# Prompt attention: the two half additions of a finished output move from VectorE to GpSimd

## The reference

```python
o_c = jnp.einsum('bqkgn,bnkd->bqkgd', p_c.astype(vc.dtype), vc)      # compressed blocks
...
o_s = jnp.einsum('bqkgm,bkqmd->bqkgd', p_s.astype(vs.dtype), vs)     # selected blocks
...
o_w = jnp.einsum('bqkgw,bwkd->bqkgd', p_w.astype(vw.dtype), vw)      # sliding window of 512
return gates[..., 0:1] * o_c + gates[..., 1:2] * o_s + gates[..., 2:3] * o_w
```

## Time and profile before

| what | before |
| --- | --- |
| median of 3 runs | 1908.28 us |
| lowest and highest | 1908.01, 1908.91 us |
| span of the profiled execution | 1907.2 us |
| PE busy over the span | 97% |
| DVE, ACT, POOL busy over the span | 61%, 48%, 25% |
| prompt attention | about 714 to 1199 us of the span |
| in 720 to 1200 us: PE, DVE, ACT, POOL busy | 465.78, 437.71, 410.18, 262.20 us of 480 |

### The profile page before, as it was taken

One profiled execution on the slowest core, in us unless ns is written; L12 is line 12 of the kernel. 1 busy time (PEld: TensorE's weight loads), 2 busy tenths in 40 slices (PEclk: granted clock), 3 DMA queues, 4 the chain that ended last, 5 costly groups with the idle time before them and its releaser, 6 DMA issues.

```text
span 1907.2 us, 31779 instructions
## 1 busy us (share of the span) xinstructions
PE 1856.5 (97%) x11644; PEld 1663.7 (87%) x11645; DVE 1164.8 (61%) x1628; ACT 917.4 (48%) x1536; POOL 481.8 (25%) x643
## 2 busy tenths in 40 slices
PE   8999999999999999999999999999989999999997
PEld 8999988899999988889888898998857888888884
DVE  5544355642212359998999989644467587644756
ACT  3243330211210358888888888311123576645755
POOL 0000000000000215555555554002111244322333
PEclk9999999999999979999999999999988999999998
DMA  5234252232313410000000000524254798877865
GB/s 173 82 109 120 78 173 56 67 113 89 113 52 86 133 31 1 1 2 1 2 2 1 2 2 12 173 72 174 83 211 159 276 393 293 293 280 238 317 225 189
DMA packets 113735, 232.60 MB, mean 122 GB/s; under 512 B 25034, under 2 KB 81906, under 8 KB 107442
## 3 DMA queue, kind: packets, MB, share of 16 engines
q1 hardware_dynamic: 106162, 205.81, 30.5%
q0 software_dynamic: 7456, 25.17, 5.2%
HBM read 190.33 MB, written 42.71 MB: 122 GB/s over the span
## 4 chain that ended last, share of the span: by engine, by line
PE 53%; DVE 4%; ACT 3%; issue 1%; POOL 1%; DMA 0%; ACTq 0%; POOLq 0%; DVEq 0%
PE ps L3020 20%; PE ps L2069 6%; PE ps L2048 5%; PE ps L2690 5%; PE ps L254 4%; PE ps L2023 3%; PE ps L2025 3%; PE ps L3008 1%; DVE small L2133 1%; PE ps L2015 1%; PE ps L3069 1%; ACT turned_high L2238 1%; PE ps L2074 1%; PE ps L2676 1%; ACT region_w L2227 1%
## 5 line engine op out<-in xcount | busy, mean ns | idle before, releaser
L2133 DVE TENSOR_REDUCE small<-ps 128x1 f32<-128x640 f32 (+7 forms) x256 | 179.8, 703 | 26.3 <-PE ps L2015 24.4
L2157 DVE TENSOR_TENSOR turned_low<-ps,turned_high 128x512 fp32r<-128x512 f32 (+2 forms) x304 | 176.6, 614 | 12.0 <-ACT turned_high L2238 8.4
L2312 POOL TENSOR_SCALAR region_w<-region_w,small,gates 128x640 f32<-128x640 f32 (+7 forms) x172 | 141.7, 834 | 131.5 <-DVE small L2137 131.5
L2238 ACT CAST turned_high<-ps 128x512 fp32r<-128x512 f32 (+2 forms) x304 | 155.0, 531 | 31.6 <-PE ps L2048 28.2
L2023 PE MATMUL ps<-key_stacks,query_stacks 128*128 128x256 f32 (+3 forms) x384 | 142.0, 370 | 15.9 <-ACT region_w L2227 8.7
L2069 PE MATMUL ps<-turned_high,value_stacks 128*128 128x256 f32 (+1 forms) x608 | 152.1, 286 | 0.0
L2069 PE MATMUL ps<-turned_low,value_stacks 128*128 128x256 f32 (+1 forms) x608 | 142.2, 279 | 0.0
L2227 ACT ACTIVATE region_w<-ps,small 128x640 f32<-128x640 f32 (+7 forms) x172 | 121.7, 708 | 24.8 <-DVE small L2133 20.1
L3020 PE MATMUL ps<-gate_parts,rows_parts 128*128 128x512 f32 x552 | 131.7, 394 | 0.0
L3020 PE MATMUL ps<-down_parts,hidden_parts 128*128 128x512 f32 x552 | 131.1, 393 | 0.0
L3020 PE MATMUL ps<-up_parts,rows_parts 128*128 128x512 f32 x552 | 128.9, 389 | 0.0
(11 more groups left out here) (507 smaller groups left out, 4978.0 us busy)
## 6 DMA issues: line engine op xcount, KB each, us to landing
region_k<-in_w_gate SPq DMA_DIRECT2D x16, 2048.0 KB, 9.6
region_k<-in_w_up SPq DMA_DIRECT2D x16, 2048.0 KB, 10.1
region_w<-in_w_down SPq DMA_DIRECT2D x16, 2048.0 KB, 12.7
region_w<-in_w_in SPq DMA_DIRECT2D x16, 512.0 KB, 4.3
small<-gate_a SPq DMA_DIRECT2D x8, 516.0 KB, 3.4
region_w<-gate_b SPq DMA_DIRECT2D x8, 516.0 KB, 3.8
region_k<-in_x_prompt SPq DMA_DIRECT2D x8, 512.0 KB, 8.1
region_k<-in_w_in SPq DMA_DIRECT2D x8, 512.0 KB, 4.4
```

The lines of the kernel that those rows point to most:

```text
L2133: nc.vector.tensor_reduce(nmax[:, n % 4:n % 4 + 1], sc, AX.X, ALU.max, negate=True).then_inc(s_max, 1)
L2157: nc.vector.tensor_tensor(lo, m.ps[:, turn_bank(G), 0:w], hi, ALU.subtract).then_inc(s_lo, 1)
L2238: nc.scalar.copy(hi, m.ps[:, turn_bank(G), 0:w]).then_inc(s_hi, 1)
L2312: nc.gpsimd.tensor_scalar(probs(H, t), probs(H, t), rec[:, H % 4, t:t + 1], m.gates[:, 2 * p + t, col:col + 1], ALU.mult, ALU.mult).then_i ...
```

## The change

The two additions of each output leave VectorE's program and enter GpSimd's. On GpSimd they stand at the same H, behind `scale(H + 1)` and `queries`, and each is followed by a wait for its own completion (a stop). The first of them signals a new semaphore `s_o0`, the second `s_o`. Before the first stand waits for GpSimd's own latest scaling and its own latest low part of queries. The last output is likewise added by GpSimd, behind its loop, and no longer by VectorE behind `low_outputs(4)`.

```diff
-    s_pv, s_ot, s_o = lw.s_values, lw.s_half, lw.s_output
+    s_pv, s_ot, s_o, s_o0 = lw.s_values, lw.s_half, lw.s_output, m.sem("a_output_low_rows")
...
-        def output(n):
-
-            j, p, _, _ = half(4 * n)
-            at, _ = queries_at(p, j)
-            dve.wait_ge(s_ot, n + 1)
-            for g in range(NKV):
-                last = nc.vector.tensor_tensor(m.RO[rows[g], at], out_kept[rows[g], g * 256:g * 256 + 256],
-                                               m.RO[rows[g], at], ALU.add)
-            last.then_inc(s_o, 1)
-
...
-            if H >= 6 and H % 4 == 2:
-                output(H // 4 - 1)
...
-        output(NHALF // 4 - 1)
...
+        def output(n):
+
+            j, p, _, _ = half(4 * n)
+            at, _ = queries_at(p, j)
+            pool.wait_ge(s_ot, n + 1)
+            nc.gpsimd.tensor_tensor(m.RO[LO, at], out_kept[LO, 0:256], m.RO[LO, at], ALU.add).then_inc(s_o0, 1)
+            pool.wait_ge(s_o0, n + 1)
+            nc.gpsimd.tensor_tensor(m.RO[HI, at], out_kept[HI, 256:512], m.RO[HI, at], ALU.add).then_inc(s_o, 1)
+            pool.wait_ge(s_o, n + 1)
+
...
             if refill(H):
                 queries(refill(H)[1], refill(H)[0])
+            if H >= 6 and H % 4 == 2:
+                pool.wait_ge(s_scaled, scaled_of[H + 1, 1] + (scaled_behind(H + 1) is not None))
+                if refill(H):
+                    pool.wait_ge(s_ql, 4 * (refill(H)[0] - 1) + refill(H)[1] + 1)
+                output(H // 4 - 1)
+        output(NHALF // 4 - 1)
```

## The result

The changed kernel takes 1930.03 us in the median of four runs (1926.77 to 1931.37), beside 1908.6 (1908.01 to 1910.76) of the kernel before on the same chip. The ratio is 1.0105, interval [1.0091, 1.012], so 20 us more. That it would be slower was forecast, and by 13.1 us, with a range that ended at 1929. The profiled execution is the one of 1931.37 us.

The account below looks back on a forecast made before the run. TensorE was taken as nearly full, VectorE close behind, with GpSimd's scaling already last at some turns. 6.3 + 6.5 + 1.0 - 0.7 = 13.1 us brought the span to 1920.3, the median to 1921.4; range 1909 to 1929.

Parts of the forecast that it names:

- VectorE's relief: Work ahead of row maxima: 0.65 us at A, 0.24 at B, 6.5 in all, swallowed; rival that it is passed on, 0.09.
- Price of an output: On GpSimd behind the queries: two additions of 0.73 us and three stops of 0.09, 1.73 in all.
- 0.35 given back: GpSimd's scaling ahead of the new additions gets 0.35 us shorter at each place once VectorE's additions leave.
- Place A: First of four output places in a head: next scaling 1.05 us late, TensorE loses all, 6 times, 6.3.
- later waits "give nothing back": Behind the turn at A: waits shift along and recover nothing; rival that 0.9 of each 1.05 is recovered, 0.12.
- the collision with L2126: Rival at A: VectorE's L2126 meets the delayed scaling, 0.35 us each, 2.1 more, at most 4.1; above 1929 us, 0.06.
- Place B: Second output place in a head: next scaling 0.93 us late, no slack, TensorE loses 0.93, 7 times, 6.5.
- Place C: Third output place in a head: next scaling 0.42 us late, slack 0.28, TensorE loses 0.14, 7 times, 1.0.
- D: Fourth output place in a head: GpSimd idles 2.77 us before its next scaling, more than 1.73, so no loss.
- the last head: Head j = 7, no queries behind A and B: gains 0.45 us at A and 0.24 at B, 0.7 together.
- The last output: Behind GpSimd's loop: the 0.95 us wait goes, GpSimd needs 1.64 where VectorE needed 0.85; gain and loss cancel, 0.
- the case above it: Tail above 1929 us, chance 0.06; additions of 1.05 us each would give 1934.

Follow-up runs that it names:

- e1: The kernel before with the two additions of each output left out on every engine: ratio 0.9898, attention 6.6 us shorter; its whole time can't be used.
- e4: The changed kernel with L2126, the subtraction of the compressed scores' row maximum, replaced by a tiny operation for odd jobs: 1924.71 us, ratio 1.0079.
- e2: The kernel before, VectorE's additions kept, plus equal additions with stops on GpSimd at the change's places, into a spare buffer nobody reads: 1928.24 us, ratio 1.0092.
- e10: The changed kernel with only the last output put back on VectorE: 1928.19 us, ratio 1.0103.
- e3: The changed kernel with GpSimd's additions one pass later (H % 4 == 3) at all four places of a head: 1918.53 us, ratio 1.0046.
- e8: The changed kernel with one GpSimd addition of 128 rows per output, without its own-instruction waits there, and ScalarE copying in two shifted pieces: 1913.59 us, ratio 1.0016.
- e6: The kernel before with VectorE's additions moved behind the pass's second row maximum and its compressed sum: 1921.89 us, ratio 1.0067.
- e5: The changed kernel with GpSimd's additions one pass later, behind the scaling, at A, B and C, unchanged at D: 1905.77 us, ratio 0.9982.

## Why the prediction was right or wrong

- **VectorE's relief, 6.5 us, swallowed at the turns: right.** e1 has 6.6, 6.0 of it behind the first addition, with less at A and more at B than forecast. In the changed kernel the waits before L2023 fell while those before turns rose, and nothing of the relief arrives at A and B.
- **Price of an output, 1.73 on GpSimd, and 0.35 given back: right.** Additions of 724 and 730 ns, scaling back at 0.99 and 1.42, the next scaling 1.08 late at A for a forecast of 1.05.
- **Place A, 6 x 1.05: the step that failed.** It measured 10.8 us for 6.3. In the prediction's words, the turn at A "loses 1.05" and the later waits "give nothing back". Two things were missing. First the collision with L2126: the turn is 1.49 late and not 1.05, 0.42 each by e4, 2.5 in all. It was among the rivals, at 0.35 each, and belonged in the sum: both instructions' rows lay there, and their times overlapped by the working itself. Second the clock, which was in no rival: in four heads it falls at the wait of 2.24 or right behind it. These heads lose 2.09 on average, and head 4, where it stays, 1.34, so 4 x 0.75 = 3.0. Head 6 loses 1.06, but it loses 0.28 less than head 4 in e4 too, so it is no measure for the others. e2 and e10 agree: the undisturbed heads but head 6 lose 1.34 to 1.36 there. Against both, the turn is 1.47 late (1.05 and 0.42), and heads lose 1.34, head 6 1.06, so that 0.13 is given back behind it, 0.41 in head 6, 1.0 in all. 6.3 + 2.5 + 3.0 - 1.0 = 10.8. So the step that later waits give nothing back was nearly right.
- **Place B, 7 x 0.93: right**, 6.6 for 6.5. **Place C, 7 x 0.14: too small**, 1.8 for 1.0. **D and the last head: right**, 0 and -0.8.
- **The last output, 0: wrong, 0.9.** GpSimd's addition was priced at 0.73 there, though VectorE's L519 with two SBUF inputs runs beside it. It took 1.36, and with that the chain to TensorE is 0.6 longer.
- **The range** ended at 1929, and the case above it had 0.06. The measured ratio puts the change at 20 us, 1928.3 from the old median; the four runs' own median is 1930.0. The bound took in the collision's full price and left the clock out.
- **The reading of the shared port.** The prediction took 0.35 as the price of VectorE's two additions and called that agreement with a full block. Both run together for 0.64 us there, so it is only half of what a block from start to end would cost. The last section has what the rows show of it.
- **Left open.** What decides whether the clock falls: behind 2.24 it did in four heads of six, in e10 likewise (2.25 to 2.27), behind 1.82 in two of six, behind 1.72 (e2) in four of six, behind 1.85 (e3) in one of seven, behind the 1.28 of place B and the 0.75 of e8 never. So the length of the wait alone doesn't decide it. GpSimd's two additions without the stop between them weren't tried. That L2126 and the scaling overlap because of the delay is shown, and that e4 takes the 0.42 away too; e4's smaller number of clock falls could be chance.

## What to carry to other kernels

An engine that is busy a quarter of the span (and 55% of this stretch, 262.20 of 480 us in the earlier trace rows) can still be the last thing that the bound engine waits for: before work is moved to it, look at what stands next in its queue and at the slack of that, place by place. The same two additions cost 20 us ahead of the scaling and gained 3 to 4 behind it, and where they went to the other side of a neighbour without such a look (e3, e6) they lost again. And when a term of the sum shifts an instruction, lay the shifted times beside the other engines' rows before adding up: two collisions of this case stood in rows that had been read.

## What the hardware showed that I had not expected

- GpSimd's two-input operation over 256 columns takes 0.73 us on 64 rows and 0.74 on 128 (e8), and 0.61 with the same tile as both inputs (e2).
- Where GpSimd's work and a VectorE instruction with two SBUF inputs overlap, both grow: L2126 from 0.68 to 1.02 and the two scalings beside it from 1.42 to 1.82; an addition beside L519 from 0.73 to 1.36; L2165 beside a scaling from 0.83 to 1.45 (e6). The Trainium skill (SBUF — State Buffer, Who interferes with whom) states an exclusive lock on the shared port pair, with the second comer fully blocked. Instruction by instruction the rows come near to that. As a rule the one that began first takes its usual time, and the other grows by the time for which both run, less 0.13 to 0.16 us. At A, L2126 grows by 0.34 of 0.49 beside the first scaling, and the second scaling by 0.41 of 0.55 beside L2126. The last output's addition grows by 0.64 of 0.77. In e5, L2126 grows by 0.17 of 0.31 and an addition by 0.33 of 0.46. In e8 an overlap of 0.15 costs neither side anything. Two kinds of row go against the order. In the kernel before, the second of VectorE's additions begins 0.22 behind a scaling and takes its usual 0.42, and the scaling pays 0.36 for both additions (0.64 together). In e2 a scaling begins 0.08 ahead of the same softmax step and still pays 0.49, and that step 0.03.
- A wait of 2.24 us on TensorE at A came in four heads of six with a stretch at the 1.2 GHz level, which cost 0.75 us on average by the heads' lengths, a third of the wait again. In e3 one such stretch cost 1.6.
